# A seven-product matrix stage on Trainium2: three PSUM banks that change their part from pair to pair, and a down weight laid out one product later

## The reference

```python
h2 = rmsnorm(x, norm2_g[l])
gate = jnp.einsum('bsd,df->bsf', h2, w_gate[l])
up = jnp.einsum('bsd,df->bsf', h2, w_up[l])
x = x + jnp.einsum('bsf,fd->bsd', jax.nn.silu(gate) * up, w_down[l])
```

## Time and profile before

| what | value |
|---|---|
| median of 3 runs | 3676.12 us (3675.49 to 3677.59) |
| the profiled execution's own time | 3679.37 us |
| its span from first to last instruction | 3677.6 us |
| TensorE busy | 3512.9 us, 96% of the span |
| VectorE busy | 2129.1 us, 58% |
| GpSimd busy | 1754.2 us, 48% |
| ScalarE busy | 1148.8 us, 31% |
| mean granted TensorE clock | 0.984 of full speed |

### The profile page before, as it was taken

How to read it: one execution, slowest core, us unless ns; L and a number is a source line. 1 busy time by engine, 2 the same in 40 slices (tenths; PEclk the granted TensorE clock), 3 DMA queues, 4 the chain that set the end, 5 groups by cost and what they waited for, 6 DMA issues and landing times.

```text
span 3677.6 us, 51937 instructions
## 1 busy us (share of the span) xinstructions
PE 3512.9 (96%) x22042; PEld 2934.5 (80%) x22042; DVE 2129.1 (58%) x2739; ACT 1148.8 (31%) x1913; POOL 1754.2 (48%) x1260
## 2 busy tenths in 40 slices
PE   8999999988999999999999999999999899999998
PEld 7788888867778787877878888777788778787876
DVE  7845566377364545456774466657778255545454
ACT  2122212266222222223122122336666222222223
POOL 4332334549255555556333324632588245545454
PEclk9999999999999999999999999999999999999999
DMA  3111313554101111113111132361231201101111
GB/s 124 36 36 36 143 52 102 176 144 140 58 23 54 50 53 51 54 50 144 46 35 36 35 149 81 121 211 58 64 108 57 72 23 37 67 35 69 36 68 64
DMA packets 79690, 275.82 MB, mean 75 GB/s; under 512 B 9057, under 2 KB 9313, under 8 KB 76900
## 3 DMA queue, kind: packets, MB, share of 16 engines
q1 hardware_dynamic: 70816, 242.25, 19.7%
q10 hardware_dynamic: 8642, 30.24, 2.1%
HBM read 224.23 MB, written 48.23 MB: 74 GB/s over the span
## 4 chain that ended last, share of the span: by engine, by line
PE 76%; DVE 14%; ACT 4%; POOL 3%; issue 2%; DMA 0%; SPq 0%; POOLq 0%; DVEq 0%; ACTq 0%
PE ps L1429 21%; PE ps L1430 20%; PE ps L1431 20%; PE ps L1435 4%; PE ps L1730 2%; PE ps L1700 2%; PE ps L1701 2%; PE ps L1735 2%; DVE acc L2127 1%; DVE af_hi_p L2126 1%; DVE tf_lo_p L2126 1%; ACT wd_hi L1784 1%; DVE af_lo_p L2126 1%; PE ps L1505 1%; DVE rhf L2126 1%
## 5 line engine op out<-in xcount | busy, mean ns | idle before, releaser
L2721 POOL TENSOR_TENSOR ring_lo<-ring_raw,ring_hi 128x512 fp32r<-128x512 f32 (+1 forms) x362 | 613.6, 1700 | 377.3 <-ACT ring_hi L1784 367.2
L1429 PE MATMUL ps<-a_hi,ring_hi 128*128 128x512 f32 x1472 | 590.7, 401 | 29.5 <-DVE af_hi_p L2126 16.5
L1430 PE MATMUL ps<-a_lo,ring_hi 128*128 128x512 f32 x1472 | 577.3, 392 | 0.0
L1431 PE MATMUL ps<-a_hi,ring_lo 128*128 128x512 f32 x1472 | 576.9, 392 | 0.0
L1429 PEld LDWEIGHTS ps<-a_hi,ring_hi 128*128 128x128 f32 x1472 | 278.5, 189 | 103.9 <-DVE af_hi_p L2126 24.1
L1431 PEld LDWEIGHTS ps<-a_hi,ring_lo 128*128 128x128 f32 x1472 | 278.5, 189 | 60.5
L1430 PEld LDWEIGHTS ps<-a_lo,ring_hi 128*128 128x128 f32 x1472 | 278.9, 189 | 54.3
L2126 DVE TENSOR_TENSOR xres<-xres,ps 128x512 f32<-128x512 f32 x352 | 234.8, 684 | 149.4 <-PE ps L1431 147.4
L1429 PE MATMUL ps<-wd_hi,af_hi 128*128 128x512 f32 x704 | 277.8, 395 | 23.4 <-DVE xres L2126 17.5
L2722 POOL TENSOR_SCALAR ring_hi<-ring_raw 128x1024 fp32r<-128x1024 f32 x84 | 108.5, 1291 | 360.3 <-PE ps L1431 311.3
L1430 PE MATMUL ps<-wd_lo,af_hi 128*128 128x512 f32 x704 | 276.6, 393 | 0.0
(11 more groups left out here) (305 smaller groups left out, 8055.9 us busy)
## 6 DMA issues: line engine op xcount, KB each, us to landing
ring_raw<-w SPq DMA_DIRECT2D x92, 512.0 KB, 3.5
ring_raw<-wgu SPq DMA_DIRECT2D x68, 512.0 KB, 3.6
uq<-q_scr SPq DMA_DIRECT2D x96, 256.0 KB, 4.8
ring_raw<-wd SPq DMA_DIRECT2D x34, 512.0 KB, 3.6
ring_raw<-wo SPq DMA_DIRECT2D x32, 512.0 KB, 3.6
uk<-k_scr SPq DMA_DIRECT2D x6, 2048.0 KB, 10.4
rlf<-wgu SPq DMA_DIRECT2D x20, 512.0 KB, 4.5
xraw<-xt SPq DMA_DIRECT2D x16, 512.0 KB, 7.4
```

Of the source, the lines that this page charges most:

```text
L1429: pe.matmul(o, ah, bh, start=begin and i == 0, stop=False)
L1430: pe.matmul(o, ah, bl, start=False, stop=False)
L1431: last = pe.matmul(o, al, bh, start=False, stop=end and i == len(pairs) - 1)
L2721: tt = lambda o, a, b, op: pool.tensor_tensor(o, a, b, op=op)
```

## The change

1. A counter `turn` goes up with each pair. The three banks 0, 1, 2 get the parts b0, b1, b2 in an order that moves by one each pair: b0, b1, b2 = turn, turn + 1, turn + 2 modulo 3. b11 and t1 use b0, t4 uses b1, b21 and t3 use b2. Bank 3 keeps its part. The engines' steps take the bank number from the plan.
2. A counter `step` goes up with each product. The down-weight jobs of groups 1 to 10 are "held": once the upper step of such a job is emitted, `split_next` does nothing more until the next product. So upper wd0 goes out with t2; lower wd0 and upper wd1 with t3; lower wd1, and then forms k0 and k1 of the next pair, with t1. No caller passes `must`.

```diff
-    wide = {"forms": None, "raw": Place(name="raw3")}
+    wide = {"forms": None, "raw": Place(name="raw3"), "turn": 0, "step": 0}
...
-    def split_next():
+    def split_next(must=False):
+        if half and not must and jobs[half[0]].get("held") == wide["step"]:
+            return False
         lower()
...
         half.append(n)
+        if "held" in j["eng"]:
+            j["held"] = wide["step"]
...
-                    ("act", ("pool", "dve")[m], "later"), wide=True)
+                    ("act", ("pool", "dve")[m], "later") + ("held",) * bool(g), wide=True)
...
         def prod(p, k, b, free):
+            wide["step"] += 1
             yield from getform(name, k)
...
-        free = yield from take(BK[0])
+        b0, b1, b2 = ((wide["turn"] + i) % 3 for i in range(3))
+        wide["turn"] += 1
+        free = yield from take(BK[b0])
         while ("t", 1) not in marks:
             yield False
-        yield from prod("b11", 0, 0, free)
+        yield from prod("b11", 0, b0, free)
...
-        emit("wino_u", hf, x, key, grab(wide["u"]), (wide["u"].ap, wide["v"].ap))
-        BK[0].free = [("wino_u", hf, *key)]
+        emit("wino_u", hf, x, key, b0, grab(wide["u"]), (wide["u"].ap, wide["v"].ap))
+        BK[b0].free = [("wino_u", hf, *key)]
...
-        free = yield from take(BK[1])
-        yield from prod("t4", 1, 1, free)
+        free = yield from take(BK[b1])
+        yield from prod("t4", 1, b1, free)
...
-        free = yield from take(BK[2])
-        yield from prod("b21", 2, 2, free)
+        free = yield from take(BK[b2])
+        yield from prod("b21", 2, b2, free)
...
-        free = yield from take(BK[2])
-        yield from prod("t3", 4, 2, free)
+        free = yield from take(BK[b2])
+        yield from prod("t3", 4, b2, free)
...
-        free = yield from take(BK[0])
-        yield from prod("t1", 5, 0, free)
+        free = yield from take(BK[b0])
+        yield from prod("t1", 5, b0, free)
```

More of the change, by code:

```diff
@@ L868, in plan_seven @@
         yield from claim(0)
-        free = yield from take(BK[1])
-        yield from prod("t4", 1, 1, free)
+        free = yield from take(BK[b1])
+        yield from prod("t4", 1, b1, free)
         yield True
-        free = yield from take(BK[2])
-        yield from prod("b21", 2, 2, free)
-        emit("wino_11", hf, x, key)
-        BK[2].free = [("wino_c", hf, *key, 0, 0)]
+        free = yield from take(BK[b2])
+        yield from prod("b21", 2, b2, free)
+        emit("wino_11", hf, x, key, b2)
+        BK[b2].free = [("wino_c", hf, *key, 0, 0)]
         yield True
@@ L882, in plan_seven @@
         yield from claim(1)
-        free = yield from take(BK[2])
-        yield from prod("t3", 4, 2, free)
-        emit("wino_21", hf, x, key, grab(wide["v"]))
-        BK[2].free = [("wino_s", hf, *key, "v")]
-        BK[1].free = [("wino_c", hf, *key, 1, 0)]
+        free = yield from take(BK[b2])
+        yield from prod("t3", 4, b2, free)
+        emit("wino_21", hf, x, key, b1, b2, grab(wide["v"]))
+        BK[b2].free = [("wino_s", hf, *key, "v")]
+        BK[b1].free = [("wino_c", hf, *key, 1, 0)]
         settled()
@@ L891, in plan_seven @@
             yield False
-        free = yield from take(BK[0])
-        yield from prod("t1", 5, 0, free)
-        emit("wino_22", hf, x, key)
-        BK[0].free = [("wino_c", hf, *key, 1, 1)]
+        free = yield from take(BK[b0])
+        yield from prod("t1", 5, b0, free)
+        emit("wino_22", hf, x, key, b0)
+        BK[b0].free = [("wino_c", hf, *key, 1, 1)]
         wide["u"].free, wide["v"].free = [("wino_s", hf, *key, "12")], [("wino_c", hf, *key, 1, 1)]
@@ L1973, in scalar @@
             elif kind == "wino_u":
-                hf, x, key, held, (U, _) = a
+                hf, x, key, b, held, (U, _) = a
                 for mark in new("act", held + [("wino", hf, *key, "b11")]):
                     act.wait_ge(*at(*mark))
-                copy(U, PS[0][:, :]).then_inc(*up("wino_u", hf, *key))
+                copy(U, PS[b][:, :]).then_inc(*up("wino_u", hf, *key))
             elif kind == "claim":
@@ L2526, in vector @@
             elif kind == "wino_u":
-                uv = a[4]
+                uv = a[5]
             elif kind == "claim":
@@ L2533, in vector @@
             elif kind == "wino_11":
-                hf, x, key = a
+                hf, x, key, b2 = a
                 for mark in new("dve", [("wino_u", hf, *key), ("wino", hf, *key, "b21")]):
                     dve.wait_ge(*at(*mark))
-                tt(made(x, key, 0, 0), uv[0], PS[2][:, :], ALU.add).then_inc(*up("wino_c", hf, *key, 0, 0))
+                tt(made(x, key, 0, 0), uv[0], PS[b2][:, :], ALU.add).then_inc(*up("wino_c", hf, *key, 0, 0))
                 finish(hf, x, key, 0, 0)
@@ L2545, in vector @@
             elif kind == "wino_21":
-                hf, x, key, held = a
+                hf, x, key, b1, b2, held = a
                 for mark in new("dve", held + [("wino_s", hf, *key, "u"), ("wino", hf, *key, "t3")]):
                     dve.wait_ge(*at(*mark))
-                tt(uv[1], uv[0], PS[2][:, :], ALU.add).then_inc(*up("wino_s", hf, *key, "v"))
+                tt(uv[1], uv[0], PS[b2][:, :], ALU.add).then_inc(*up("wino_s", hf, *key, "v"))
                 for mark in new("dve", [("wino_s", hf, *key, "v")]):
                     dve.wait_ge(*at(*mark))
-                tt(made(x, key, 1, 0), uv[1], PS[1][:, :], ALU.subtract).then_inc(*up("wino_c", hf, *key, 1, 0))
+                tt(made(x, key, 1, 0), uv[1], PS[b1][:, :], ALU.subtract).then_inc(*up("wino_c", hf, *key, 1, 0))
                 finish(hf, x, key, 1, 0)
             elif kind == "wino_22":
-                hf, x, key = a
+                hf, x, key, b0 = a
                 for mark in new("dve", [("wino", hf, *key, "t1")]):
                     dve.wait_ge(*at(*mark))
-                tt(made(x, key, 0, 1), uv[0], PS[0][:, :], ALU.add).then_inc(*up("wino_s", hf, *key, "12"))
-                tt(made(x, key, 1, 1), uv[1], PS[0][:, :], ALU.add).then_inc(*up("wino_c", hf, *key, 1, 1))
+                tt(made(x, key, 0, 1), uv[0], PS[b0][:, :], ALU.add).then_inc(*up("wino_s", hf, *key, "12"))
+                tt(made(x, key, 1, 1), uv[1], PS[b0][:, :], ALU.add).then_inc(*up("wino_c", hf, *key, 1, 1))
                 lower(hf, x, key, 1, 0)
```

## The result

**The changed kernel took 3644.56 us** (median of 4 runs, 3642.5 to 3646.13), the kernel before 3675.8 (4 runs, 3671.37 to 3677.59). The ratio is 0.9915, with a 95% interval of 0.9903 to 0.9926. The forecast was 3646 us, range 3641 to 3659. The profiled execution took 3646.13 us (span 3644.4) against 3679.37 (span 3677.6); the mean granted clock is 0.984 in both.

The account below looks back on a forecast made before the run. TensorE, three quarters of the last-ending chain, was taken to lose 1.42 us per group to a late VectorE. Terms 6.4 + 19.8 + 3.4 - 1.2 + 3.2 - 0.9 made 30.7; 30 off the median gave 3646 us, range 3641 to 3659.

Parts of the forecast that it names:

- In front of b22 and b11: TensorE's waits before these two products go: 20 x 0.32 = 6.4 us and 18 x 1.10 = 19.8 us won.
- Form k0's margin: Next pair's b11 form, just in time after B (t1's start): 0.05 us lost per group, -0.9 in all.
- The late DMA: Two b11 places where k0's load came late: 3.4 us won, 1.2 us of waiting left.
- `down(10)`: Its wait for af_lo of result 21 goes, 1.6 us in each half, 3.2 us won.
- The price of wd_lo: VectorE's wd_lo at its new place takes 1.22 us with GpSimd idle; 2.88 us is the other bound.
- The banks: Bank 0 in time by 0.7 us even without rotation; rotation gives a margin if wd_lo takes 2.88 us.
- The detail for half 0: First pair starts on late-freed bank 2; b11 may lose up to 2.72 us before a 6.9 us wait; booked 0.
- What is late next: First xres must free bank 4 for the fifth down tile, due 13.6 us after t1 begins; 0.5 us to spare.
- Number 1: GpSimd's low part of k0 is late, as wd_lo holds it up or k0 lands late: 13 us back, 3659; 10%.
- Number 2: The fifth down tile waits for xres after a missed GpSimd slot: 21 us back, 3667; 7%.
- Number 3: Slower: wd_lo lands ahead of the gate product on VectorE, b11's load loses 2.3 us, 3692; 3%.
- Number 4: The change does nothing: both waits stay since b11 was waiting for its form; 2%.

Follow-up runs that it names:

- the later low half alone: The changed kernel with fixed banks, keeping only wd_lo moved one product later: 3645.16 us; 3647.17 us when measured again.
- half of the hold: The changed kernel with only wd1 held back, not wd0, and the banks still rotating: 3659.92 us.
- the engines exchanged: The kernel before, with wd0's low part on VectorE and wd1's on GpSimd in groups 1 to 10, no hold, fixed banks: 3664.8 us.
- the low half made twice: VectorE makes wd1's low part twice in a row: 3667.56 us with the hold and fixed banks, 3664.55 us in the changed kernel.
- part 1 alone: The changed kernel with fixed banks, so only the low part is one product later: 3645.16 us, 3647.17 us again.
- the later t1 steps: Hold with fixed banks, and the steps making group 1's t1 operand put off to the third row tile of down(0): 3636.7 us, again 3639.89 us.

## Why the prediction was right

**The terms of the sum.** It was 30.7 us against the profiled execution, which came out 33.2 lower. Between the medians it is 31.2, where 30 was booked; the parts outside the change gave the trace 1.2 us more (2.2 less 1.0), which is chance. The time alone doesn't confirm both edits: the later low half alone, 3645.16, meets the same forecast.

- *In front of b22 and b11* (6.4 and 19.8): the waits are gone in all 20 and all 18 places. Nine groups of half 0 take 59.84 each, as 264 matmuls should, against the 61.28 that the earlier trace rows gave.
- *Form k0's margin* (-0.9): the chain af_hi, k0, GpSimd ran at B+2.44, B+2.98, B+3.67, within 0.02 us of what was worked out, and the 0.05 per group was not lost. Cost: 0.
- *The late DMA* (3.4 won, -1.2 left): it was there once, not twice, in half 1 (so too in the second trace of this kernel, 60.29 us; with fixed banks it was there twice). ScalarE had k0 0.55 us later than usual, and the group took 60.19 (3127.92 to 3188.11), 0.35 more than 59.84:

```profile
3128.03 0.63 ACT L1791 ACTIVATE af_hi<-af_lo_p 128x512 fp32r<-128x512 f32 x1 [3.11 <-DVE af_lo_p L2133]
3129.12 0.63 ACT L1791 ACTIVATE ring_hi<-ring_raw 128x512 fp32r<-128x512 f32 x1 [0.45 <-DMA ring_raw<-wgu]
```

  That is how small the new kernel's margin is: half a microsecond of a late load costs a third of one. These two terms, over-cautious by 1.8 together, explain most of the difference between the 26.9 that the sum gave for the groups (without its last two b22 waits) and the 29.05 measured.
- *`down(10)`* (3.2): the `af_lo` wait of 1.5 is out of both halves; half 1's end came 1.87 sooner, where 1.6 and one b22 wait make 1.92.

**The price of wd_lo.** Of the bounds 1.22 and 2.88, 1.22 held in all 20 groups. The reason given, that it makes no progress while GpSimd runs, now rests on more rows. The blocked instruction ended 1.09 us behind GpSimd's instruction before, 1.07 behind it with half of the hold, and 1.07 behind a `ring_lo` with the engines exchanged. The other direction was shown by the low half made twice. That is what the Trainium skill, "SBUF — State Buffer", section "SBUF: two separate sides", states: whoever starts first has the shared ports for its whole instruction. The trace agrees in both directions, with these numbers.

**The banks.** "With part 1 alone this would be in time too" was right: with fixed banks no group waited for bank 0. The step that failed is the case kept for the rotation: "the rotation gives a margin if wd_lo takes 2.88". With 2.48 us of wd_lo, form k0 was as late as bank 0, and with it b11, whatever the bank. It cost the forecast nothing, since wd_lo took 1.22. The detail for half 0 came true as a 1.8 us wait of the first pair (`af_lo_p`); with the `xres` wait behind it 8.4 us were lost there, as before (1.5 for `af_lo` and 6.9).

**What is late next.** The first `xres` is done near B+12.9 (estimate: the first of the three in the row at 1205.80), 0.7 before it is due, where 0.5 was forecast.

**The rivals.** Number 1 (GpSimd held up, 3659) did not occur, but its mechanism is real: a block of 2.48 brings it, for more than I had priced (3667.56), since `xres` waits come with it. Number 2 (`xres`) did not occur either, and is what nearly cancels the banks' work when they are changed alone. Number 3, slower, had no place: wd_lo stood behind the gate product. Number 4 (nothing) is excluded.

## What to carry to other kernels

An instruction that waits for its input at the head of an in-order engine delays everything behind it by its wait and its own length, so find the engine's idle place that is late enough for the input and early enough for the consumer, and check who else uses the memory ports there. When a wait is taken away in one place, look for the same engine's next deadline before booking the gain: changing the banks removed a real wait of 0.8 to 1.8 us and brought 0.13 us per group, because the same VectorE was due again 8 us later. And where the trace names a releaser that ended just when the wait did, a variant that doesn't need it tells whether it was the cause.

## What was not expected of the hardware

- VectorE and GpSimd block each other for whole instructions in both directions. VectorE's 128x1024 subtraction took 1.22, 1.47, 2.88 or 3.33 us, by where it fell against GpSimd's; GpSimd's own took 2.39 before and 2.85 after, where it started at 1192.32 inside a VectorE subtraction (`af_lo`, until 1192.91). VectorE's additions that read PSUM kept their 0.67 to 0.69 us beside a busy GpSimd.
- After TensorE had waited 6.62 us, until 1084.48, the granted clock was still 0.50 (1.2 of 2.4 GHz) between 1088 and 1090. After 4.62 us, until 1080.02, it fell too, but was back at 1.00 some four microseconds later. The length of the wait alone does not set this: in the kernel with the later low half alone it was back 4.6 us behind a wait of 6.9, until 1081.41. Behind the 1.8 us stall of the kernel before it had been 0.50 as well. Against the kernel with the later low half alone, the shorter wait gave back more than its own length: 2.3 us less of waiting made the stretch from the first to the second low part of wd1 2.8 us shorter. The rest is about what 3.4 us of matmuls at half clock cost less than 4.6 (0.6, an estimate from the two traces). Two windows of the changed kernel and of the one with the later t1 steps:

```profile
1088.00:1090.00 2.00, 2.00 (x6) 1.55 (x5) 0.96 (x2) 1.06 (x1) 2.00 (x2) 0.50 0.00 0
```

```profile
1082.00:1084.00 2.00, 2.00 (x6) 1.54 (x5) 0.69 (x1) 0.00 (x0) 2.00 (x2) 0.51 0.00 0
1084.00:1086.00 2.00, 2.00 (x10) 1.68 (x9) 0.69 (x1) 0.00 (x0) 1.92 (x3) 1.00 0.00 0
```
